# The split of a weight unit on GpSimd: pieces of 256 columns in place of one instruction

## The reference

```python
for i in range(DEPTH):                                   # 4
    sh1, sc1, g1, sh2, sc2, g2 = ada_mod(cond, w_ada[i], b_ada[i])   # silu(cond) @ w_ada + b_ada
    h = modulate(x, sh1, sc1)                            # rms_norm(x) * (1 + scale) + shift
    m = fourier_mix(h, w_fnet) | pool_mix(h, w_pool, scale) | mla(h, ...)
    x = x + g1 * m
    h = modulate(x, sh2, sc2)
    u = dwconv3(h @ w_in, w_conv, b_conv)                # w_in: 1024 x 5632
    gate, val = split(u)
    x = x + g2 * ((silu(gate) * val) @ w_out)            # w_out: 2816 x 1024
y = rms_norm(x) * g_final                                # outputs: y of both groups, MLA state
```

## Time and profile before

| | us |
|---|---|
| median of three runs (lowest, highest) | 2904.91 (2898.97, 2906.93) |
| the profiled execution | 2902.93 |
| its span in the trace | 2901.1 |
| busy: PE | 2647.5 (91%) |
| busy: DVE | 1581.9 (55%) |
| busy: ACT | 941.4 (32%) |
| busy: POOL | 835.4 (29%) |

### The profile page before, as it was taken

How to read it: one execution, slowest core, us unless ns; L and a number is a source line. 1 busy time by engine, 2 the same in 40 slices (tenths; PEclk the granted TensorE clock), 3 DMA queues, 4 the chain that set the end, 5 groups by cost and what they waited for, 6 DMA issues and landing times.

```text
span 2901.1 us, 45482 instructions
## 1 busy us (share of the span) xinstructions
PE 2647.5 (91%) x17182; PEld 2600.7 (90%) x17182; DVE 1581.9 (55%) x2661; ACT 941.4 (32%) x1388; POOL 835.4 (29%) x356
## 2 busy tenths in 40 slices
PE   6889999996499999998898899899999978999998
PEld 6879999996399999988788889899999878999998
DVE  7577546476874574663443433763646776313235
ACT  3234223133432231342332333432313434313232
POOL 0012333334423333332111012233333302333332
PEclk9989999998699999999988898999999999999999
DMA  7433334342043343422110011242433311222222
GB/s 261 151 124 126 128 115 147 109 150 86 30 144 117 116 146 115 145 89 70 44 37 31 30 44 66 101 139 95 148 128 133 116 59 61 77 73 72 73 73 80
DMA packets 83862, 293.48 MB, mean 101 GB/s; under 512 B 9952, under 2 KB 13472, under 8 KB 83360
## 3 DMA queue, kind: packets, MB, share of 16 engines
q1 hardware_dynamic: 77184, 281.05, 28.4%
q10 hardware_dynamic: 6560, 10.79, 1.1%
HBM read 288.88 MB, written 2.93 MB: 101 GB/s over the span
## 4 chain that ended last, share of the span: by engine, by line
PE 78%; DVE 11%; ACT 4%; issue 3%; DMA 2%; POOL 1%; ACTq 0%; SPq 0%; DVEq 0%
PE acc L555 73%; PE sacc L555 2%; DMA raw<-in_stream 2%; PE sacc L749 2%; DVE rows L1734 1%; DVE x L1705 1%; DVE products L1747 1%; DVE rows L1572 1%; DVE pt_lo L1620 1%; DVE h_lo L1566 1%; POOL w_lo L430 1%; ACT w_hi L1034 1%; PE acc L944 1%; DVE conv L1797 0%; DVE scratch L1976 0%
## 5 line engine op out<-in xcount | busy, mean ns | idle before, releaser
L430 POOL TENSOR_TENSOR w_lo<-raw,w_hi 128x1024 fp32r<-128x1024 f32 (+2 forms) x287 | 709.2, 2472 | 1756.9 <-ACT w_hi L1034 1756.9
L555 PE MATMUL acc<-h_hi,w_hi 128*128 128x322 f32 x2944 | 930.6, 316 | 102.4 <-DVE x L1725 29.4
L555 PE MATMUL acc<-h_lo,w_hi 128*128 128x322 f32 x2944 | 924.4, 314 | 0.0
L555 PE MATMUL acc<-h_hi,w_lo 128*128 128x322 f32 x2944 | 923.5, 314 | 0.0
L555 PEld LDWEIGHTS acc<-h_hi,w_hi 128*128 128x128 f32 x2944 | 563.9, 192 | 113.3 <-issue 71.1
L555 PEld LDWEIGHTS acc<-h_lo,w_hi 128*128 128x128 f32 x2944 | 566.7, 192 | 0.5 <-issue 0.4
L555 PEld LDWEIGHTS acc<-h_hi,w_lo 128*128 128x128 f32 x2944 | 562.7, 191 | 0.0
L1034 ACT ACTIVATE w_hi<-raw 128x1024 fp32r<-128x1024 f32 (+2 forms) x287 | 296.4, 1033 | 806.8 <-PE acc L555 766.5
L1747 DVE SCALAR_TENSOR_TENSOR products<-raw,cond 128x1024 f32<-128x1024 f32 x324 | 412.9, 1312 | 12.0 <-ACT cond L1501 10.9
L555 PE MATMUL acc<-g_hi,w_hi 128*128 128x322 f32 x1168 | 366.0, 313 | 10.0 <-POOL w_lo L430 8.0
L555 PE MATMUL acc<-g_hi,w_lo 128*128 128x322 f32 x1168 | 362.8, 311 | 0.0
(11 more groups left out here) (201 smaller groups left out, 3585.5 us busy)
## 6 DMA issues: line engine op xcount, KB each, us to landing
raw<-in_stream SPq DMA_DIRECT2D x536, 512.0 KB, 3.3
x<-in_x ACTq DMA_DIRECT2D x8, 322.0 KB, 10.4
cond<-in_cond ACTq DMA_DIRECT2D x2, 1024.0 KB, 6.1
inv_count<-in_inv_count ACTq DMA_DIRECT2D x1, 1328.0 KB, 5.8
out_y<-y ACTq DMA_DIRECT2D x2, 644.0 KB, 4.3
out_y<-y ACTq DMA_DIRECT2D x8, 161.0 KB, 2.5
rows<-in_rope ACTq DMA_DIRECT2D x1, 644.0 KB, 3.8
conv_w<-in_conv_w ACTq DMA_DIRECT2D x4, 88.0 KB, 2.4
```

Of the source, the lines that this page charges most:

```text
L430: nc.gpsimd.tensor_tensor(lo, raw[slot][:, 0:raw_size], hi.bitcast(f32), ALU.subtract).then_inc(unit_done[slot], 1)
L555: done = nc.tensor.matmul(o, lhs[lp], rhs[rp][half], start=first and z == 0, stop=last and z == 2)
```

## The change

`cut` issues a loop of `tensor_tensor` instructions over pieces of at most 256 columns; the last of them raises `unit_done[slot]`. A unit of 1024 columns gives four instructions, one of 768 three, one of 512 two. The wait for `weights_hi` stands once, before the first. What is computed and where it is written is the same, and so are the programs of all other engines. Lines after the new ones are up to three higher in the changed kernel: the cut is L433, the loop of the FFN L487.

```diff
 UNIT = 1024
+QUARTER = UNIT // 4
 SLOTS = 4
...
             def cut(slot, split, hi, lo, raw_size):
                 pool.wait_ge(weights_hi, split + 1)
-                nc.gpsimd.tensor_tensor(lo, raw[slot][:, 0:raw_size], hi.bitcast(f32), ALU.subtract
-                                        ).then_inc(unit_done[slot], 1)
+                for first in range(0, raw_size, QUARTER):
+                    cols = slice(first, min(first + QUARTER, raw_size))
+                    done = nc.gpsimd.tensor_tensor(lo[:, cols], raw[slot][:, cols], hi[:, cols].bitcast(f32), ALU.subtract)
+                done.then_inc(unit_done[slot], 1)
```

## The result

Over 20 runs each, the changed kernel takes 2911.14 us and the kernel before 2905.34: a ratio of 1.0022 with a 95% interval of 1.0012 to 1.0031. It is slower by some 6 us. The interval excludes that nothing changed. It reaches to just over 0.3%, so a difference under 0.3% is likely and not certain. Its profiled execution takes 2912.88 us, 9.95 more than the one before, so the two profiles show a larger difference than the medians do.

What follows compares the result with a forecast made beforehand. The prediction took PE, busy 91% of the span, to bound the kernel. Its terms 7.8 + 1.2 + 0.5 - 0.1 + 0.8 made +10.2 us on 2904.91, about 2915 us, range 2904 to 2924.

Steps and rivals of the forecast that it cites:

- A: Project with extra ada units, layers 0 to 2: DVE products between pieces lengthen PE's waits for a cut, +7.8 us.
- F: The FFN loop itself, with most of the cuts: cover absorbs the longer cuts, no new PE wait, 0 us.
- B: First tile of the FFN loop, four layers: the cut ends later than DVE's conv, +1.2 us.
- C: Norm before the FFN: layer 2's squares gain 2.2 us, layers 0, 1 and 3 lose, together +0.5 us.
- D: MLA latents: +0.45 at PE's wait at 1321, -0.8 at DVE's square at 1333, in all -0.1 us.
- E: Smaller starts: attention's first head, last fnet layer's tables, pool mixing, two projection ends; +0.8 us.
- (1): Rival: queued pieces follow so closely that DVE gets no turn; 2909 to 2913 us, chance 0.12.
- (2): Rival: third-tile cost smaller, one product slipping in or pieces near 0.64 us; 2909 to 2912 us, chance 0.18.
- (3): Rival: DVE's waits are what counts, pieces give time back at squares and latents; about 2901 us, chance 0.08.
- (4): Rival: the FFN loop's cover breaks, PE waits in some 50 tiles; about 2965 us, chance 0.05.

Runs made afterwards that it cites:

- f1: Kernel before with only the cut for the third tile of project's first turn, layers 0 to 2, in four pieces; 2915.55 us, ratio 1.0033.
- f2: Changed kernel with only the three third-tile cuts of project, layers 0 to 2, whole again; 2903.32 us, ratio 0.9995 to the kernel before.
- g3: Kernel before with 256-column pieces only in latent cuts at 1332, 1358, 1377, layer 2's second pair and the last fnet layer; 2886.44 us, ratio 0.9945.
- g4: Changed kernel with all cuts in pieces of 128 columns, eight for a unit; 2938.32 us, ratio 1.0120 to the kernel before.
- e1: Kernel before with only the third cut that project itself makes, layers 0 to 2, in four pieces; 2905.39 us, ratio 1.0009.

## Why the prediction was right, point by point

**A, the third tile (7.8 us).** Right in place (but for its name), sign and mechanism. The waits grew by 2.40, 2.40 and 2.39 where 2.6 was said; a piece takes 0.70 us from start to start where 0.70 was taken (the lower bound of 0.64, with a fixed part of 0.085 us, came from the `h_lo` row and is wrong). Mis-sized is what lies behind the wait: the sum has no term for the clock. f1 measures the three places alone at 9.6 us, and its profile has 9.1 at them, that of the changed kernel 9.6.

**F, the loop (0).** Right: the cover held, no new wait appeared, and the long stretches of the loop differ by 0.01 us or less. It even held by more than was said. The rows that answer to the earlier trace rows, POOL and DVE:

```profile
309.58 3.40 POOL L433 TENSOR_TENSOR w_lo<-raw,w_hi 128x256 fp32r<-128x256 f32 x4 [4.28 <-ACT w_hi L1037]
...
312.29 1.77 DVE L1750 SCALAR_TENSOR_TENSOR products<-raw,cond 128x1024 f32<-128x1024 f32 x1
```

The trace runs 1.69 us ahead of the one before here, so the product asks at 313.98 of its time and the fourth piece began near 313.9: the cut was through first, the product waited 0.5 us, and none slipped in.

**B (1.2 us).** The waits grew by 2.9 (0.8, 0.8, 0.9, 0.3), of which the longer cut can explain 0.3 to 0.4 each. The rest comes without any pieces as well: f1, with whole cuts there, waits +1.0, -0.1 and +1.6 us more at the first three, and the six kernels with whole cuts +0.5 to +1.6 at the first. Two profiles can't tell a term of 1 us from that. Only layer 3's is alike in every kernel, +0.3 with pieces of 256 and 0.0 with whole cuts.

**C (0.5 us).** The step that failed: the gain was too small, two of the losses too large. Layer 2's squares gave 2.72 us of waiting and 3.6 in all, for 2.2. Layer 3 lost 0.4, for 1.0. Layer 0 lost nothing that can be told, for 1.0: PE's wait there is 8.0 to 9.3 us in four kernels with pieces of 256, 8.2 to 9.6 in seven with whole cuts. Layer 1 was right, +0.8 for 0.7: a wait shorter by 0.5 and one longer by 1.3 stand in all four kernels with pieces and in none with whole cuts. By the waits C was about -1.5 and not +0.5.

**D and E (0.7 us).** Waits of the latents -0.9, for -0.1; +0.42 at 1321 and -0.94 at 1333 as written (+0.45, -0.8). Of E the tables cost 0.07, for 0.2, and the first head nothing, for 0.3. What has no term is the last fnet layer, where two waits for DVE (`h_lo` and the nyquist rows) are 1.2 us shorter.

**The sum.** All but A was put at +2.4; f2 measures it at -1.5 (-4.9 to +2.3). A was put at 7.8 and is 9.6. The two errors cancel in part, 10.2 forecast against 5.8 by medians and 6.4 by the ratio, inside the range but some 40% below the forecast. By the middle of the interval that is on the other side of the 0.3% line: the likeliest class, slower with 0.51, was missed by little, and "the same" had 0.44. That the time is so near is in part luck, since a term at nothing (the clock behind the waits) and a sum that was too high elsewhere cancel. That the profiled pair differs by 9.95 is luck as well: 5.3 of it are no waiting, mostly the clock in one execution each.

**The rivals.** (1) is refuted by the two products' 1.39 and 1.73 us between the pieces, and its lower price of a piece by the 0.70. (2)'s total was nearly met, but not for its reason: two products slip in, and it is the other places that are cheaper. (3) has the right places: layer 2's squares give back more than it says (2.7 us for 2.2), the latents' squares about as much (1.3 for 1.2), the norms of layers 0, 1 and 3 nothing. g3 is that rival without A; its 3.2 us less waiting are of (3)'s size, its 16 us are not, and most of them are the clock, which (3) does not speak of. (4)'s point of decision was right, and g4 shows what lies beyond it: not 1 us at each of 50 tiles but 0.3 to 0.7 at one pair of tiles in two.

## What to carry to other kernels

Where two engines exclude each other for an instruction, its length is how long the other may wait, and the number of pieces is how often it may step in: cut short what the bounding engine does not wait for, and leave whole what it does. So decide it instruction by instruction: 3 of 328 cuts made this change slower, and pieces in 9 others alone made the kernel 16 us faster than it was, though only about 3 us of that are the waits for which they were chosen. And a wait of the bounding engine has a second price or gain in its clock, which a sum of waits does not see. Before you put a number on that, look at several executions: two traces here differ by 6 us in one stage by the clock, with nothing changed in it or just ahead of it.

## What was not expected of the hardware

PE's wait of 5.03 us at 2140.67 left the granted clock at 0.50 for the next 4 us of matmuls; the wait of 2.64 us at the same tile before left it at 1.00. But the same wait of 2.65 and 2.69 us in the other two layers did not: over eight kernels the clock was at 0.50 behind 12 of 24 such waits, with 1.3 to 1.5 us lost, behind all 9 of 5.03 to 5.09 us, with 1.5 to 1.9 us lost, and behind none of the 3 of 0.60 to 0.81 us. What decides it for the waits of 2.65 us is open.

In the attention stage, with waits equal within 0.5 us in sum, the same matmuls ran at 0.88 or at 1.00 where only three cuts of the stage before had been changed, 13.8 us in all between two traces; the trace of e1 has 6.5 us of such a difference with no cut of the two stages changed.

A product and a piece of a cut alternate, also with the next cut's pieces queued behind: in pieces of 128 columns, 0.42 us apart when alone, two products of 1.15 us lay within three of them. A subtraction on GpSimd costs 0.14 us for each instruction beside 2.16 ns a column, from 128 to 1024 columns.
